# Sparse attention in a decoder layer: a third slot for page chunks, and the next pair's bias strips made at tile 2

## The reference, cut to what matters

```python
s = jnp.einsum('btghd,bcgd->bghtc', qg, kcmp) * scale + bias     # compressed blocks
sq = jnp.einsum('bqghd,bgqsd->bghqs', qb, kg) * scale + bsel     # selected blocks (all keys up to the query, masked)
s = jnp.einsum('bnqghd,bnkgd->bnghqk', qb, kb) * (N_HD ** -0.5) + bias   # sliding window of 512
o = g[:, :, :, 0] * o_cmp + g[:, :, :, 1] * o_sel + g[:, :, :, 2] * o_win
```

## Time and profile before

| | us |
|---|---|
| median of 3 runs | 2271.54 (2266.53 to 2273.16) |
| the profiled execution, its own time | 2278.08 |
| its span, first to last instruction | 2276.1 |
| TensorE matmul busy | 2167.6 (95% of the span) |
| VectorE busy | 1286.7 (57%) |
| ScalarE busy | 846.6 (37%) |
| GpSimd busy | 621.8 (27%) |

### The profile page before, as it was taken

How to read it: one execution, slowest core, us unless ns; L and a number is a source line. 1 busy time by engine, 2 the same in 40 slices (tenths; PEclk the granted TensorE clock), 3 DMA queues, 4 the chain that set the end, 5 groups by cost and what they waited for, 6 DMA issues and landing times. The chain is left out here.

```text
span 2276.1 us, 42843 instructions
## 1 busy us (share of the span) xinstructions
PE 2167.6 (95%) x17101; PEld 1981.1 (87%) x17101; DVE 1286.7 (57%) x2350; ACT 846.6 (37%) x1720; POOL 621.8 (27%) x523
## 2 busy tenths in 40 slices
PE   9999998988988989999999999999899999999997
PEld 6799977866555579999999988899899999999997
DVE  5214253356675671132337154567899887876957
ACT  5222253136655650011243133553333433334443
POOL 5000035402222211122011300241344433445643
PEclk9999998889999999999999999998999999999998
DMA  4321197963443431111310155232223232265234
GB/s 144 108 65 47 21 225 229 312 235 120 145 146 115 160 107 42 64 53 42 132 42 34 58 228 233 79 131 85 90 104 109 74 120 90 87 234 188 91 121 148
DMA packets 133714, 276.35 MB, mean 121 GB/s; under 512 B 24626, under 2 KB 79571, under 8 KB 128332
## 3 DMA queue, kind: packets, MB, share of 16 engines
q1 hardware_dynamic: 110796, 232.32, 30.6%
q0 software_dynamic: 10368, 28.33, 3.8%
q10 hardware_dynamic: 12352, 12.96, 1.8%
HBM read 229.49 MB, written 48.26 MB: 122 GB/s over the span
## 5 line engine op out<-in xcount | busy, mean ns | idle before, releaser
L88 PE MATMUL psum<-merged_high,oq_half 128*128 128x352 f32 x768 | 189.1, 326 | 1.8 <-POOL oq_half L69 1.4
L88 PE MATMUL psum<-ff_t,ff_x_slots 128*128 128x264 f32 x1200 | 149.1, 284 | 1.4 <-DVE ff_x_slots L69 1.4
L88 PEld LDWEIGHTS psum<-ff_t,ff_x_slots 128*128 128x128 f32 x1200 | 147.1, 188 | 1.7 <-issue 1.6
L88 PEld LDWEIGHTS psum<-merged_high,oq_half 128*128 128x128 f32 x768 | 135.2, 190 | 2.5 <-POOL oq_half L69 1.9
L1698 POOL DMA_DIRECT2D na_kv<-in_pool x128 | 69.2, 541 | 225.2 <-PE psum L1902 156.6
L88 PE MATMUL psum<-x_half_high,mg_w_high 128*128 128x352 f32 x384 | 124.0, 323 | 2.0 <-ACT gated L2383 1.2
L88 PE MATMUL psum<-h_again_low,mg_w_high 128*128 128x352 f32 x384 | 123.1, 321 | 0.0
L88 PE MATMUL psum<-x_half_high,mg_w_low 128*128 128x352 f32 x384 | 123.0, 320 | 0.0
L2000 ACT ACTIVATE na_pt<-psum 128x512 f32<-128x512 f32 (+1 forms) x170 | 86.5, 543 | 90.3 <-PE psum L1875 81.8
L88 PE MATMUL psum<-ff_bslot,ff_x_slots 128*128 128x264 f32 x888 | 117.3, 285 | 0.7 <-DVE ff_z L4348 0.7
L69 POOL TENSOR_TENSOR ff_x_slots<-low,ff_x_slots 128x512 fp32r<-128x512 f32 x52 | 82.2, 1595 | 114.1 <-ACT ff_x_slots L3796 108.8
(11 more groups left out here) (671 smaller groups left out, 5620.8 us busy)
## 6 DMA issues: line engine op xcount, KB each, us to landing
na_kv<-in_pool SPq DMA_DIRECT2D x128, 128.0 KB, 3.6
na_kv<-in_pool POOLq DMA_DIRECT2D x128, 128.0 KB, 4.2
ff_bslot_raw<-mid_ops SPq DMA_DIRECT2D x59, 264.0 KB, 3.1
mid_ops<-ff_bufs SPq DMA_DIRECT2D x11, 1056.0 KB
mg_w<-in_w_merge SPq DMA_DIRECT2D x15, 768.0 KB, 4.4
ring<-in_f_wu SPq DMA_DIRECT2D x11, 1024.0 KB, 5.4
low<-in_f_wg SPq DMA_DIRECT2D x22, 512.0 KB, 4.5
first_pages<-in_pool SPq DMA_DIRECT2D x68, 128.0 KB, 5.7
```

Of the source, the lines that this page charges most:

```text
L88: ins = nc.tensor.matmul(out, w[a], x[b], start=first and n == 0, stop=last and n == 2)
```

## The change

A third slot `kv2` of the same size is added, and its semaphores. Chunk m lies in slot m % 3. At the item of chunk m both queues wait for the same event as before, the values of chunk m, and issue chunk m+3. Chunk 2 needs no wait: SyncE issues its half behind chunk 0 and the strip of pair 1, ahead of chunk 1 (which waits for the own bias); GpSimd issues its half right after the gates, ahead of its walk through the items. The return of `hm` into slot 0 comes at the item of chunk 15 instead of chunk 16. GpSimd makes the next pair's strips at the item SEL of tile 2 instead of tile 7.

```diff
         kv = (tile_at("na_kv0", [P, 4, 2 * CH], hm_at), kv1)
+        kv = (*kv, sb("kv2", [P, 4, 2 * CH]))
+        NKV = len(kv)
...
-        filled = lambda m, size: sum(size(j) for j in range(m % 2, m + 1, 2))
+        filled = lambda m, size: sum(size(j) for j in range(m % NKV, m + 1, NKV))
 
         def slot_free(eng, m):
 
-            if m >= 2:
-                eng.wait_ge(S["pv_ready"], order[chunk_items[m - 2]] + 1)
+            if m >= NKV:
+                eng.wait_ge(S["pv_ready"], order[chunk_items[m - NKV]] + 1)
             elif m == 0:
                 eng.wait_ge(S["hm_kept"], 16)
-            else:
+            elif m == 1:
                 eng.wait_ge(S["scores_ready"], logits_done(at[OWN_BIAS, 0, 0]))
...
             load_chunk(0)
             load_strip(1)
+            load_chunk(2)
             for u in range(U):
...
                 if br == PAGES:
-                    m = chunk_of[u] + 2
+                    m = chunk_of[u] + NKV
                     if m < len(chunk_items):
                         load_chunk(m)
-                    elif m % 2 == 0:
+                    elif m % NKV == 0:
                         slot_free(sp, m)
                         sp.dma_start(hm, A["hm_spill"]).then_inc(S["hm_back"], 16)
...
+            load(pool, 2, POOL_PAGES, kv_soft)
             for u in range(U):
                 br, p, t = items[u]
-                if br == SEL and t == NTILE - 1 and p + 1 < NPAIR:
+                if br == SEL and t == 2 and p + 1 < NPAIR:
                     other_strips(p + 1)
-                if br == PAGES and chunk_of[u] + 2 < len(chunk_items):
-                    load(pool, chunk_of[u] + 2, POOL_PAGES, kv_soft)
+                if br == PAGES and chunk_of[u] + NKV < len(chunk_items):
+                    load(pool, chunk_of[u] + NKV, POOL_PAGES, kv_soft)
```

More of the change, by code:

```diff
@@ L1671, in sparse_attention @@
         S = {n: sem(n) for n in names}
-        kv_loaded = [sem(f"kv_loaded{j}") for j in range(2)]
+        kv_loaded = [sem(f"kv_loaded{j}") for j in range(NKV)]
         strip_loaded = [sem(f"strip_loaded{j}") for j in range(2)]
-        kv_soft = [N["soft"][f"n{j}"] for j in range(2)]
+        kv_soft = [N["soft"][f"n{j}"] for j in range(NKV)]
         block = ctx.enter_context(nc.Block())
@@ L1697, in load @@
             for (b, p), g in zip(mine, page):
-                eng.dma_start(kv[m % 2][:, b, 2 * PAGE * p:2 * PAGE * (p + 1)],
-                              A["pool"][ds(g, 1), :, 2 * PAGE:4 * PAGE].rearrange("a p x -> (a p) x")).then_inc(done[m % 2], 16)
+                eng.dma_start(kv[m % NKV][:, b, 2 * PAGE * p:2 * PAGE * (p + 1)],
+                              A["pool"][ds(g, 1), :, 2 * PAGE:4 * PAGE].rearrange("a p x -> (a p) x")).then_inc(done[m % NKV], 16)
         @block.sync
@@ L1708, in load_chunk @@
                 for b in range(4):
-                    sp.dma_start(kv[m % 2][:, b, :].rearrange("p (k x) -> p k x", k=2), A["winp"][4 * s + b]
-                                 ).then_inc(kv_loaded[m % 2], 16)
+                    sp.dma_start(kv[m % NKV][:, b, :].rearrange("p (k x) -> p k x", k=2), A["winp"][4 * s + b]
+                                 ).then_inc(kv_loaded[m % NKV], 16)
             def load_strip(p):
@@ L1770, in page_keys @@
             def page_keys(m, b):
-                x = kv[m % 2][:, b, :]
+                x = kv[m % NKV][:, b, :]
                 return x[:, 0:CH] if chunk(m)[2] == WINDOW else x.rearrange("p (a x) -> p a x", x=2 * PAGE)[:, :, 0:PAGE]
@@ L1775, in page_value @@
                 c = CH + j * P if chunk(m)[2] == WINDOW else 2 * PAGE * j + PAGE
-                return kv[m % 2][:, b, c:c + P]
+                return kv[m % NKV][:, b, c:c + P]
             def scores(u):
@@ L1786, in scores @@
                     m = chunk_of[u]
-                    pe.wait_ge(kv_loaded[m % 2], filled(m, hard))
+                    pe.wait_ge(kv_loaded[m % NKV], filled(m, hard))
                     if filled(m, soft):
-                        pe.wait_ge(kv_soft[m % 2], filled(m, soft))
+                        pe.wait_ge(kv_soft[m % NKV], filled(m, soft))
                 for n in pieces_of[u]:
@@ L4626, in build @@
             N = {"n_pool": A["pool"].shape[0],
-                 "soft": {n: ctx.enter_context(nc.semaphore(n)) for n in ("c0", "c1", "n0", "n1")}}
+                 "soft": {n: ctx.enter_context(nc.semaphore(n)) for n in ("c0", "c1", "n0", "n1", "n2")}}
             N.update({n: ctx.enter_context(nc.semaphore(n)) for n in ("w1_ahead", "C_ahead", "kv_ahead")})
```

## The result

The changed kernel took 2258.96 us (median of 11 runs, 2254.96 to 2267.38), the kernel before on the same chips 2274.35 us (11 runs, 2266.53 to 2280.28). The ratio is 0.9937, with a 95% interval of 0.9921 to 0.9953: faster by 0.63%, some 14 us (15.4 between the medians), where 17.4 were forecast. The profiled execution took 2256.59 us, span 2254.6. Lines of `sparse_attention` moved down by 2 to 4: L1821 is now L1825, L1875 is L1879, L2149 is L2153, L1748 is L1751; in e4, e5 and e7 to e9 they lie up to 4 lines further down.

What follows compares the result with a forecast made beforehand. TensorE's order of work was taken to bound the stage, with 42.3 us idle and its clock to win. 9.0 + 4.8 + 3.6 = 17.4 us off the median 2271.54 gave 2254 us, range 2246 to 2264.

Steps and rivals of the forecast that it cites:

- Part 1: Third slot: all ten TensorE page waits (16.3 us) go, 9.0 us won after waits for VectorE's scaling; bounds 7.0 and 16.3.
- Part 2: TensorE's clock: three half-clock falls behind the longest page waits go, 4.8 us won; bounds 0 and 4.8.
- Rival (a): TensorE's clock falls elsewhere as often; gain 12.6 us, time 2259; chance 0.15.
- Part 3: Strips at the three pair boundaries: three TensorE waits for ScalarE's copy go, 3.6 us won; bounds nothing and 8.1.
- a held VectorE: GpSimd's strip copies holding VectorE's scaling over shared ports: cost taken as 0; as a rival 6.3 us lost, chance 0.06.
- Part 4: Start and end of the stage: chunk 2's early load delays chunks 0 and 1 harmlessly; cost 0, bounds 0 and 3 us.
- Rival (d): VectorE keeps its whole boundary lead, 8.1 for 3.6 us, and CLOSE 0's stall halves; gain 24, time 2247.5; chance 0.12.

Runs made afterwards that it cites:

- e4: Changed kernel with the values put ahead of the turning where a chunk's scores stand before them; 0.9912 of the kernel before, 2251.75 us.
- e5: e1 with 9 of a chunk's 16 page DMAs on SyncE and 7 on GpSimd instead of 8 and 8; 0.9930 of the kernel before.
- e7: Changed kernel with chunk 2 loaded later, behind the scores of OWN_BLOCKS on both queues; 0.9936 of the kernel before.
- e9: e5 with the split turned round, 9 of a chunk's page DMAs on GpSimd and 7 on SyncE; 0.9965 of the kernel before.
- e1: Changed kernel (three slots) with the strips made at tile 7 again; 0.9970 of the kernel before.
- e6: e1 with only the last pair's strips made at tile 2; 0.9934 of the kernel before.
- e3: Changed kernel with the strips made at tile 5 instead of tile 2; 0.9935 of the kernel before.
- e8: e4 with CLOSE 0 after tile 2 of its pair and its three sums at the second, fourth and sixth item; 0.9892 of the kernel before, 2249.29 us.

## Why the prediction was right

The sum was 17.4 us, the stage gave 15.8 and the medians 15.4; 2254 was forecast, 2259 came, inside the range. Of the 5 us between, 2.8 are the base: the forecast took off from 2271.54, and the kernel before had a median of 2274.35 over 11 runs.

- **Part 1** held as worked out. All ten page waits went, and the wait for the scaling that showed in their place was 0.5 to 1.0 us (forecast 0.75 each, from the earlier trace rows): 8.8 for 9.0. Had the 16.3 us of the earlier trace rows been taken whole, this term would have been 7.5 us too high.
- **Part 2** held: three falls gone, 4.9 for 4.8. Rival (a), that the clock falls elsewhere, came in small: one new fall (0.9). Against that, the fall at CLOSE 0, which the forecast left as it was, was shorter by luck: it is 10.2 or 10.3 us long in the kernel before and in e1 to e5 and e7, and 6.8 in the changed kernel, e6 and e9, and none of these edits touches CLOSE 0.
- **Part 3**: the sum is as forecast, but in part by accident. 1.0 and 0.7 us came at the first and last boundary, for 1.29 and 1.03, as new waits of 0.3 to 0.4 us for L2133 and one of 0.5 for ScalarE's copy stayed; the second gave 1.9 with the shorter half-clock stretch in it. In e3, with the full 10.3 us stretch, that boundary gave 1.1, so about 2.8 us are the strips' and 0.8 the clock's. The price put at 0, a held VectorE, was 0.6.
- **Part 4** held: no page wait at chunk 0 or 1, and e7 is not faster.
- What the forecast missed altogether is that the parts depend on each other. It gave the slots 13.8 us and the strips 3.6; alone they bring about 7 and 4. It priced the slots by the loads that they move and looked at the events that the queues wait for; it did not ask what stands behind a load in GpSimd's order, nor for a queue's own pauses. GpSimd's stall by count was in the trace of before, unread, in a place where it cost nothing. The third slot put it ahead of the strips, and the strips' move took them out of its way in the same edit. That this didn't spoil the sum is luck, not foresight.
- Rival (d) failed, the stall at CLOSE 0 stayed; e8 shows what it was worth.

## What to carry to other kernels

A wait that goes uncovers the next one: price it by the place in the trace where the first is absent already. When loads are moved earlier, look at everything that stands behind them in the issuing engine's order, and at that engine's own pauses, which travel with its count of DMAs. And a wait of 2 to 3 us on TensorE can cost 1.5 to 1.6 us more in half clock, as three did here; the seven shorter page waits of the kernel before cost only themselves.

## What the runs showed that was not expected

- GpSimd stood once for 2.48 to 2.78 us between its 201st and 202nd DMA of the kernel, in each of the ten traces with that many, wherever that fell (between 708 and 754 us), and not in the one with 200. Its cause is open.
- Beside GpSimd's copies a scaling on VectorE of 0.55 us became 1.19 us long and the next 0.86 (changed kernel, pair 1), while VectorE's bias additions beside the same copies kept their 0.69 us (e3).
- In this stage, behind its first 30 us, every wait of TensorE of 2.29 us and more came with 3.4 to 6.8 us at 1.2 GHz. Waits of 1.5 to 1.9 us did so only in part: none of the four in the kernel before that stand alone (1.52, 1.57, 1.75 and 1.91), but all three of 1.9 in e9. The same wait near 518 us, 1.56 to 1.75 long, was followed by a fall in six of eleven traces, the changed kernel's among them. The two waits at CLOSE 0, 1.5 and 2.0 us within 3 us, came with 6.8 to 10.3 us at half clock in all ten traces that have them.
- The runs of the changed kernel spread by 12 us and go with the mean granted clock: 2255 to 2259 us at 0.974 and 0.975, 2262 at 0.972, 2266 and 2267 us at 0.970 and 0.969.
